# A hybrid decoder layer on one core: expert weights in a ring of ten 2 MB units, padding rows skipped, expert results scattered into the output by adding

## The chip, the cores and the metric

One core of one Trainium2 chip runs the whole layer in one launch. The metric is the device time in microseconds; three runs of the kernel before took 1293.37, 1296.27 and 1298.17 us, median 1296.27.

## The reference, cut to what matters

One layer over 512 prompt tokens and 8 sample tokens, model width 1024, all in float32. Projections, a pooling mixer, sparse attention and memory attention come first; the change touches what follows them:

```python
def finish(x, y_pool, o_nsa, o_mem, p):
    ...
    h = x + mixed @ p['w_out']
    hn = rmsnorm(h, p['g_ffn']).reshape(b * t, d)
    return h + hier_moe(hn, p).reshape(b, t, d)

def hier_moe(x, p):                      # top-1 of 4 groups, then top-2 of its 8 experts
    ...
    for gi in range(N_EXPERT_GROUPS):
        hg = jnp.einsum('nd,edf->nef', x, p['w_gate'][gi])
        hu = jnp.einsum('nd,edf->nef', x, p['w_up'][gi])
        h = jax.nn.silu(hg) * hu * combine[:, gi, :, None]
        y = y + jnp.einsum('nef,efd->nd', h, p['w_down'][gi])
    return y
```

Each of the 520 tokens goes to 2 of 32 experts, 1040 token-expert pairs in all, 32.5 an expert on average. An expert has three matrices, gate and up (1024 x 512) and down (512 x 1024), 2 MB each; the 32 experts have 201 MB.

## The kernel before

The kernel is a row of stages (`project`, `stream`, `attend`, `mix`, `experts`, `overflow`, `combine`), each a block in which every engine has its own program; the engines meet at a barrier at each stage's end (`close`). Within a stage the order on each engine is written out by hand and semaphores tie the engines.

`project` also clears the spare part of `ys_dram` with one 4 MB write of zeros from GpSimd's queue (L302). `mix` computes h and hn for five token tiles (four of 128, one of 8), stores them to `h_dram` and `hn_dram` (L1308, L1309), routes the tokens on VectorE, and makes `table` (slot by expert tile, the token in each slot; 64 slots a tile) by ten small matmuls (L1438) and one cast (L1660). Empty slots hold token 0. At its start SyncE loads the three matrices of expert 0 into `w_a` (L1297 to L1299), for the last token tile gate and up of expert 1 into `w_b` (L1306), and after the last logits its down matrix (L1317).

`experts` works on one expert n at a time with 64 rows:

- GpSimd gathers the 64 rows of hn into `xg` (L1726), one gather an expert, two buffers; gather n waits only for `x_turned` of n-2.
- TensorE runs, for each n: `gate_up(n)` (64 matmul passes, L1751), `turn_x(n+1)` (transposes of `xg`, L1739 and L1741), `down(n-1)` (16 passes, L1770), `turn_h(n)` (L1739, L1741).
- VectorE copies the transposes out (L1813, L1829) and computes the activation (L1819 to L1825), with ScalarE's exponential (L1856) between.
- ScalarE copies the result out of PSUM (L1862) and stores all 64 rows to `ys_dram` in two DMAs (L1865).
- SyncE loads gate and up of expert n+2 after the last up matmul of n, and down of n+2 after the last down matmul of n, into the half (`w_a` or `w_b`) that n leaves:

```python
sp.wait_ge(up_done, i * 4 + 2 * (slot - 1))
self.load_gate_up(sp, i * 2 + slot, slot, (wg[slot], wu[slot]))
sp.wait_ge(y_in_psum, i * 4 + 2 * (slot - 1))
self.load_down(sp, i * 2 + slot, slot, wd[slot])
```

`overflow` runs only if an expert has more than 64 rows, which these inputs don't have. `combine` gathers each token's two rows from `ys_dram` (ten gathers, L2020), multiplies each by its weight and adds it to h on VectorE (L2032, L2033), and stores the output (L2039).

Of the kernel before, what the change touches and what calls it, by code (L numbers as in the profile page):

```python
# [24 lines left out]
P = 128  # L25
# [3 lines left out]
NB = 8  # L29
# [34 lines left out]

C_ID = 0
# [16 lines left out]
CW = C_SEL + 16 * NB  # L82
# [7 lines left out]
def constants():  # L90
# [40 lines left out]
    c[:, C_TOK:C_TOK + 5] = i[:, None] + P * np.arange(5)[None, :]  # L131
    for u in range(2):
# [18 lines left out]
class Kernel:  # L151
# [35 lines left out]
    def project(self):  # L187
# [16 lines left out]
        xin2 = self.sb("xin", [P, 2, D], stack=st)  # L204
# [6 lines left out]
        blank = self.w1[0:CAP, :, :, :].rearrange("p a b c -> p (a b c)")[:, 0:D]  # L211
        blank_ready = self.sem("blank_ready", st)
# [33 lines left out]
        def _(sp):  # L246
# [21 lines left out]
            sp.wait_ge(self.blanked, 16)  # L268
# [28 lines left out]
        def _(pool):  # L297

            nc.gpsimd.memset(blank[:, :], 0.0).then_inc(blank_ready, 1)
            pool.wait_ge(blank_ready, 1)  # L300
            pool.wait_ge(win_in, 64)
            pool.dma_start(self.ys_dram[NEXP * CAP:, :].rearrange("(a p) d -> p a d", p=CAP), blank[:, :].unsqueeze(1).broadcast_to([CAP, NOVER, D])).then_inc(self.blanked, 16)  # L302
# [8 lines left out]
            pool.wait_ge(self.blanked, 16)  # L311
# [152 lines left out]
    def stream(self):  # L464
# [11 lines left out]
        XT = self.sb("XT", [P, 2, G, 512], stack=st)  # L476
# [55 lines left out]
        pTc = self.sb("pTc", [64, 64], stack=st)  # L532
# [427 lines left out]
    def attend(self):  # L960
# [15 lines left out]
        prob = self.sb("prob", [P, 2, 2, 512], stack=st)  # L976
# [275 lines left out]
    def mix(self):  # L1252
# [25 lines left out]
        place = self.sb("place", [P, 6, NT * 2], stack=st)  # L1278
        stored = [S(f"h_stored{j}") for j in range(2)]
        names = ("mix_dve", "cleared", "r_in_psum", "r_ready", "y_in_psum", "y_out", "ms_ready4", "root_ready", "mixed_ready",  # L1280
                 "mT_in_psum", "mT_ready", "h_in_psum", "hms", "hroot", "hn_ready", "hT_in_psum", "hT_ready", "l_in_psum",
                 "l_out", "lclear", "lexp", "pair_ready", "cnt_in_psum", "h_read", "h_copied", "hot_ready", "table_in_psum")
        (steps, cleared, r_in_psum, r_ready, y_in_psum, y_out, ms_ready, root_ready, mixed_ready,
         mT_in_psum, mT_ready, h_in_psum, hms, hroot, hn_ready, hT_in_psum, hT_ready, l_in_psum,
         l_out, lclear, lexp, pair_ready, cnt_in_psum, h_read, h_copied, hot_ready, table_in_psum) = (S(n) for n in names)
# [4 lines left out]
        tile_tok = mixed[:, 0, 0:2 * NT * NTILE].rearrange("p (n s) -> p n s", s=NTILE)  # L1290
# [4 lines left out]
        def _(sp):  # L1295

            wg, wu, wd = self.expert_slot(self.w_a)  # L1297
            self.load_gate_up(sp, 0, 0, (wg, wu))
            self.load_down(sp, 0, 0, wd)  # L1299
            for t in range(NT):  # L1300
                r = ROWS[t]
                if t == NT - 1:

                    wg, wu, wd = self.expert_slot(self.w_b)
# [12 lines left out]
            self.load_down(sp, 1, 1, wd)  # L1317

        @block.gpsimd
        def _(pool):  # L1320
            nc.gpsimd.memset(one[:, :, :, :], 0.0).then_inc(cleared, 1)
            nc.gpsimd.memset(cnt[:, :, :], 0.0).then_inc(cleared, 1)
            nc.gpsimd.memset(self.pair_w[:, :, :], 0.0).then_inc(cleared, 1)
            nc.gpsimd.memset(lg[:, :, :], 0.0).then_inc(cleared, 1)

        @block.tensor
        def _(pe):
# [3 lines left out]
            def windows(t):  # L1331
                r = ROWS[t]
                if t >= 1:
                    pe.wait_ge(r_ready, t)
                band = lambda w, j: bands[:, C_BAND + (3 * w + j) * P:C_BAND + (3 * w + j + 1) * P]
                for w in range(4):
                    u = z[0:r, t, U0 + 64 * w:U0 + 64 * w + 64]
# [343 lines left out]
    def experts(self):  # L1681
# [467 lines left out]
```

## Time and profile before

| what | us |
|---|---|
| median of three runs | 1296.27 (1293.37 to 1298.17) |
| span of the profiled execution, first to last instruction | 1288.5 |
| `experts` and later, from the first gather | 719.95 to 1288.5 |
| busy in the span: TensorE matmuls, VectorE, ScalarE, GpSimd | 1060.3, 458.5, 175.3, 71.2 |

The profiled execution has no time of its own beside its span; the median of the runs lies 7.8 us above the span, and that is taken as what lies around it. The weight loads run on queue q1 (SyncE's), ScalarE's stores on q10, GpSimd's gathers on q0; all three share the core's 16 DMA engines.

### The profile page before, as it was taken

Reading aid. Unit: us, or ns where it says so; the run is one execution under the profiler, and the core shown is the slowest. Engines: PE = TensorE matmul, PEld = TensorE weight load, DVE = VectorE, ACT = ScalarE, POOL = GpSimd, SP = SyncE. Lnnn points to the kernel's source line nnn. Section 1 sums busy time; section 2 is a strip of 40 time slices with the busy share of each in tenths; the row PEclk is TensorE's granted clock in tenths of the full one; section 3 lists DMA queues with packets and bytes.
Section 4 is the critical chain, followed back from the end, with each engine's and each line's share of the span. In section 5 each row is a group of like instructions: output and inputs, shape, how many; then the busy total and the mean of one; then the engine's idle time right before and its main releaser. Section 6 shows DMA issues by size and latency. Waiting matters only on the chain. (4 is left out here: it accounts for less than half of the span.)

```text
span 1288.5 us, 16001 instructions
## 1 busy us (share of the span) xinstructions
PE 1060.3 (82%) x6275; PEld 694.2 (54%) x6275; DVE 458.5 (36%) x950; ACT 175.3 (14%) x415; POOL 71.2 (6%) x104
## 2 busy tenths in 40 slices
PE   5899979999996899988996498788887788877880
PEld 2455657777784677776455354444444444444440
DVE  3233313422424678653434322222222222222223
ACT  1021211111100344330001000000000000000000
POOL 0000030100100000000000100000000000000003
PEclk9999889999976799686996698999999999999995
DMA  9970083553100600004115279999999999999995
GB/s 396 266 231 25 13 199 99 154 141 98 50 1 2 253 1 1 1 1 196 69 63 231 81 284 401 403 400 408 409 404 407 405 407 410 406 413 415 407 382 207
DMA packets 58438, 294.33 MB, mean 228 GB/s; under 512 B 6992, under 2 KB 23183, under 8 KB 40783
## 3 DMA queue, kind: packets, MB, share of 16 engines
q1 hardware_dynamic: 35191, 255.76, 51.8%
q0 software_dynamic: 5280, 21.15, 5.2%
q10 hardware_dynamic: 17920, 16.78, 4.2%
q8 instruction: 31, 0.51, 0.2%
q14 instruction: 16, 0.13, 0.0%
HBM read 272.55 MB, written 25.42 MB: 231 GB/s over the span
## 5 line engine op out<-in xcount | busy, mean ns | idle before, releaser
L1751 PE MATMUL ps<-w_b,xTe 128*64 128x256 f32 x1024 | 132.0, 416 | 37.8 <-DMA w_b<-in_w_up 34.1
L1751 PE MATMUL ps<-w_a,xTe 128*64 128x256 f32 x1024 | 123.2, 397 | 27.0 <-DMA w_a<-in_w_up 24.9
L1813 DVE COPY xTe<-ps 128x512 f32<-128x512 f32 x32 | 22.1, 692 | 345.9 <-PE ps L1741 345.9
L829 PE MATMUL ps<-XT,w_a 128*128 128x126 f32 (+1 forms) x576 | 132.9, 409 | 5.7 <-DVE ht L564 5.7
L829 PEld LDWEIGHTS ps<-XT,w_a 128*128 128x128 f32 x576 | 120.4, 227 | 15.4 <-issue 6.3
L1751 PEld LDWEIGHTS ps<-w_b,xTe 128*64 128x64 f32 x1024 | 81.4, 150 | 83.9 <-DMA w_b<-in_w_up 40.9
L1751 PEld LDWEIGHTS ps<-w_a,xTe 128*64 128x64 f32 x1024 | 74.3, 142 | 71.3 <-DMA w_a<-in_w_up 30.8
L430 PE MATMUL ps<-w_b,xT 128*128 128x454 f32 (+1 forms) x240 | 81.1, 549 | 0.7 <-ACT z L402 0.7
L1856 ACT ACTIVATE gc<-gc 128x256 f32<-128x256 f32 x32 | 13.3, 416 | 450.2 <-DVE gc L1819 450.2
L1726 POOL DMA_INDIRECT xg<-hn_dram,table x32 | 28.8, 899 | 592.6 <-PE ps L1741 453.9
L1378 PE MATMUL ps<-w_b,mT 128*128 128x512 f32 x128 | 58.1, 614 | 1.9 <-ACT mT L1446 1.3
L430 PEld LDWEIGHTS ps<-w_b,xT 128*128 128x128 f32 (+1 forms) x240 | 38.0, 172 | 39.7 <-issue 39.7
L1770 PE MATMUL ps<-w_b,hTe 128*64 128x512 f32 x256 | 58.5, 599 | 0.5 <-DVE hTe L1829 0.5
L1770 PE MATMUL ps<-w_a,hTe 128*64 128x512 f32 x256 | 58.4, 598 | 0.0
L1822 DVE RECIPROCAL gc<-gc 128x256 f32<-128x256 f32 x32 | 56.1, 1753 | 1.1
L1098 PEld LDWEIGHTS ps<-z,pT 128*128 128x128 f32 x320 | 40.9, 207 | 15.9 <-ACT pT L1238 10.2
L1098 PE MATMUL ps<-z,pT 128*128 128x64 f32 x320 | 43.7, 293 | 3.3 <-DVE pT L1204 3.1
L1739 PE MATMUL ps<-consts,hh 128*128 128x128 f32 x64 | 16.4, 338 | 34.8 <-DVE hh L1825 34.8
L1739 PEld LDWEIGHTS ps<-consts,hh 128*128 128x128 f32 x64 | 10.2, 199 | 62.2 <-DVE hh L1825 61.3
L1378 PEld LDWEIGHTS ps<-w_b,mT 128*128 128x128 f32 x128 | 24.8, 197 | 32.6 <-issue 30.9
L550 DVE COPY KsT<-ps 128x512 f32<-128x512 f32 x8 | 5.5, 692 | 101.6 <-PE ps L806 101.6
L1227 ACT ACTIVATE prob<-ps,stt 128x256 f32<-128x256 f32 (+3 forms) x80 | 40.4, 522 | 2.7 <-DVE stt L1159 2.6
(362 smaller groups left out, 1308.5 us busy)
## 6 DMA issues: line engine op xcount, KB each, us to landing
w_a<-in_w_gate SPq DMA_DIRECT2D x16, 2048.0 KB, 17.2
w_a<-in_w_up SPq DMA_DIRECT2D x16, 2048.0 KB, 23.3
w_a<-in_w_down SPq DMA_DIRECT2D x16, 2048.0 KB, 12.5
w_b<-in_w_gate SPq DMA_DIRECT2D x16, 2048.0 KB, 16.6
w_b<-in_w_up SPq DMA_DIRECT2D x16, 2048.0 KB, 22.4
w_b<-in_w_down SPq DMA_DIRECT2D x16, 2048.0 KB, 13.2
w_a<-in_cache_kv SPq DMA_DIRECT2D x64, 256.0 KB, 5.1
ys_dram<-yb ACTq DMA_DIRECT2D x64, 128.0 KB, 7.8
```

Source lines behind the costliest of these rows:

```text
L430: ins = nc.tensor.matmul(in_psum(t, a), xT[:, t % 2, k, 0:r], rhs, start=(k == 0), stop=(k == KD - 1))
L829: ins = nc.tensor.matmul(hidv[:, 2 * q:2 * q + 2, 0:n], w1[:, q, l, :], XT[:, q, :, l:l + 8 * (n - 1) + 1:8], start=(l == 0), stop=(l == 15))
L1098: ins = nc.tensor.matmul(ps[:, 6, 64 * c:64 * c + 64], pT[:, j, at:at + 128], z[:, k, v:v + 64], **add)
L1227: ins = nc.scalar.activation(pr[:, i // n, i % n, :], sc[:, i // n, i % n, :], ACT.Exp, bias=stt[:, u % 2, 1, i:i + 1], scale=SCALE, accum ...
L1378: ins = nc.tensor.matmul(ps[0:r, 4 + a, :], mT[:, k, 0:r], w_out[:, k, 512 * a:512 * a + 512], start=(k == 0), stop=(k == KD - 1))
L1726: pool.indirect_dma_start(out=xg[:, n % 2, :], out_offset=None, in_=self.hn_dram, in_offset=bass.IndirectOffsetOnAxis(ap=self.table[:, n:n ...
L1739: ins = nc.tensor.matmul(dst, src, ident, start=True, stop=True)
L1751: ins = nc.tensor.matmul(ps[h * CAP:h * CAP + CAP, bank, 0:FH], xT[:, slot, k, :], w[slot][:, k, h * FH:h * FH + FH], start=(k == 0), stop ...
L1770: ins = nc.tensor.matmul(ps[a * CAP:a * CAP + CAP, 6 + slot, :], hT[:, j, h * CAP:h * CAP + CAP], wd[slot][:, h, j, 512 * a:512 * a + 512] ...
L1813: nc.vector.tensor_copy(xT[:, slot, :, :].rearrange("p k s -> p (k s)"), ps[:, 4, 0:KD * CAP]).then_inc(xT_ready, 1)
L1822: link(nc.vector.reciprocal(gc[:, slot, :], gc[:, slot, :]), n * 3 + 2)
L1856: nc.scalar.activation(gc[:, slot, :], gc[:, slot, :], ACT.Exp, scale=-1.0).then_inc(ge_ready, 1)
```

## The change

Five things are changed together.

1. **Ring of units.** `w_a`, `w_b`, the former `z` and 4 MB more make ten units of 2 MB; unit u = 3n + m holds matrix m (gate, up, down) of expert n and lies in place u mod 10. Each unit is loaded as soon as the unit ten before it has been read. `mix` loads units 0, 1, 2, 6, 7 at its start (6 and 7 lie where z was, so GpSimd first copies 256 columns of z to `zu`, and TensorE's first matmuls and these loads wait for it), 3 and 4 at the last token tile, 5 after the last logits; `experts` loads 8 and 9 at once.
2. **Padding.** Empty slots of the table hold 2048, beyond the bound that the gather is given, so their rows aren't fetched. Slot 0 of a tile always has a row.
3. **Scatter.** ScalarE multiplies the result by the slot's weight as it copies it out of PSUM (the weights come out of the same, now doubled, table matmuls). GpSimd adds it into the output by one indirect DMA an expert, 128 half rows of 2 KB with a bound that leaves the empty slots out. `mix` stores h straight to the output.
4. **Order on GpSimd.** For each n: wait for `x_turned` of n, gather n+2, wait for `y_copied` of n and for scatter n-1 to have landed, scatter n. The first two gathers stand in `mix`.
5. **Gone**: `combine`, `ys_dram` and its clearing in `project`, the stores on ScalarE's queue, `h_dram`. `overflow` is folded into `experts`.

```diff
@@ project @@
-            pool.dma_start(self.ys_dram[NEXP * CAP:, :].rearrange("(a p) d -> p a d", p=CAP), blank[:, :].unsqueeze(1).broadcast_to([CAP, NOVER, D])).then_inc(self.blanked, 16)
@@ mix @@
-            self.load_gate_up(sp, 0, 0, (wg, wu))
-            self.load_down(sp, 0, 0, wd)
+            for u in range(3):
+                self.load_unit(sp, u)
+            sp.wait_ge(u_kept, 2)
+            for u in range(6, 8):
+                self.load_unit(sp, u)
...
-                    self.load_gate_up(sp, 1, 1, (wg, wu))
+                    for u in range(3, 5):
+                        self.load_unit(sp, u)
...
-                sp.dma_start(self.h_dram[t * P:t * P + r, :], h[0:r, t % 2, :]).then_inc(stored[t % 2], 16)
+                sp.dma_start(O["y"][t * P:t * P + r, :], h[0:r, t % 2, :]).then_inc(stored[t % 2], 16)
...
-            self.load_down(sp, 1, 1, wd)
+            self.load_unit(sp, 5)
...
+            nc.gpsimd.tensor_copy(zu[:, 0:TILES, :], z[:, 0:TILES, U0:U0 + 256]).then_inc(u_kept, 1)
+            nc.gpsimd.tensor_copy(zu[0:NB, TILES, :], z[0:NB, TILES, U0:U0 + 256]).then_inc(u_kept, 1)
...
+            pool.wait_ge(table_ready, 1)
...
+            for n in range(2):
+                self.gather(pool, n)
...
-                    ins = nc.tensor.matmul(ps[0:CAP, 0, 0:NTILE], slot_hot[0:r, n, :], tile_tok[0:r, n, :], start=(n == 0), stop=(n == 2 * NT - 1))
+                    for a in range(2):
+                        ins = nc.tensor.matmul(ps[CAP * a:CAP * a + CAP, 0, 0:2 * NTILE], slot_hot[0:r, n, :], tile_hot[0:r, n, :, :].rearrange("p m s -> p (m s)"),
+                                               start=(n == 0), stop=(n == 2 * NT - 1))
...
+            ch.then(nc.vector.tensor_tensor(weighted, hot, pw[:, :, :].rearrange("p t k -> p (t k)").unsqueeze(2).broadcast_to([P, 2 * NT, NTILE]), ALU.mult))
+            nc.vector.scalar_tensor_tensor(hot, tok[:, :].unsqueeze(2).broadcast_to([P, 2 * NT, NTILE]), -float(FAR), hot, ALU.add, ALU.mult).then_inc(hot_ready, 1)
...
+            ch.then(nc.vector.tensor_scalar(row, ps[:, 0, 0:NTILE], float(FAR), self.c(C_LAST, 1), ALU.add, ALU.min))
+            nc.vector.tensor_copy(self.table[:, :], row[0:CAP, :]).then_inc(table_ready, 1)
+            nc.vector.tensor_scalar(self.halves[:, :], row, 2.0, self.c(C_HALF, 1), ALU.mult, ALU.add)
+            nc.vector.tensor_copy(self.slot_w[:, :], ps[:, 0, NTILE:2 * NTILE])
@@ experts @@
+    def gather(self, pool, n):
+
+        pool.indirect_dma_start(out=self.xg[0:CAP, n % 2, :], out_offset=None, in_=self.hn_dram,
+                                in_offset=bass.IndirectOffsetOnAxis(ap=self.table[:, n:n + 1].bitcast(U32), axis=0),
+                                bounds_check=NTOK - 1, oob_is_err=False).then_inc(self.xg_in[n % 2], 16)
...
+        def scatter(pool, n, slot, sem):
+
+            pool.indirect_dma_start(out=rows, out_offset=bass.IndirectOffsetOnAxis(ap=self.halves[:, n:n + 1].bitcast(U32), axis=0),
+                                    in_=yb[:, slot, :], in_offset=None, bounds_check=2 * NTOK - 1, oob_is_err=False,
+                                    compute_op=ALU.add).then_inc(sem, 16)
...
+            for u in range(8, NU):
+                if u >= RING:
+                    n, m = (u - RING) // 3, (u - RING) % 3
+                    if m == 0:
+                        sp.wait_ge(gate_done, 2 * n + 2)
+                    elif m == 1:
+                        sp.wait_ge(up_done, 2 * n + 2)
+                    else:
+                        sp.wait_ge(y_in_psum, 2 * n + 2)
+                self.load_unit(sp, u)
...
             for n in range(NEXP):
-                if n >= 2:
-                    pool.wait_ge(x_turned, n - 1)
-                pool.indirect_dma_start(out=xg[:, n % 2, :], out_offset=None, in_=self.hn_dram,
-                                        in_offset=bass.IndirectOffsetOnAxis(ap=self.table[:, n:n + 1].bitcast(U32), axis=0)).then_inc(xg_in[n % 2], 16)
+                if n + 2 < NEXP:
+                    pool.wait_ge(x_turned, n + 1)
+                    self.gather(pool, n + 2)
+                pool.wait_ge(y_copied, n + 1)
+                if n >= 1:
+                    pool.wait_ge(y_out, 16 * n)
+                scatter(pool, n, n % 2, y_out)
...
+                nc.scalar.activation(yb[:, n % 2, :], ps[0:2 * CAP, 6 + n % 2, :], ACT.Copy, scale=self.slot_w[:, n:n + 1]).then_inc(y_copied, 1)
```

TensorE's order in `experts` stays, `down(n)` now waits for `y_copied` of n-2 only, and the loops are unrolled.

## Rows read from the trace of the kernel before

**Rows 1.** Windows: length, busy us of each engine, TensorE clock, DMA share, GB/s.
```profile
40.00:60.00 20.00, 20.00 (x54) 10.53 (x53) 3.78 (x8) 1.38 (x3) 0.00 (x0) 0.92 1.00 237
...
719.00:757.00 38.00, 26.78 (x175) 16.21 (x175) 8.94 (x14) 1.42 (x3) 4.59 (x5) 0.78 0.42 146
757.49:1225.57 468.08, 377.90 (x2578) 213.73 (x2577) 121.43 (x196) 28.03 (x56) 24.18 (x27) 0.96 1.01 406
1264.00:1288.50 24.50, 0.00 (x0) 0.00 (x0) 12.73 (x10) 0.00 (x0) 10.27 (x10) 0.50 0.73 261
```

**Rows 2.** Waits from 760 to 1240 us: waiter, releaser, total us, times, longest.
```profile
POOL xg L1726 <- PE ps L1741: 425.3, 27, 18.9
...
PE ps L1751 <- DMA w_b<-in_w_up: 32.8, 14, 3.1
...
PE ps L1751 <- DMA w_a<-in_w_up: 24.9, 13, 2.9
```

**Rows 3.** DMA queues from 760 to 1240 us: packets, MB, share of 16 engines.
```profile
q1 hardware_dynamic: 16068, 180.76, 92.7%
q0 software_dynamic: 2160, 7.08, 4.3%
q10 hardware_dynamic: 4640, 7.61, 4.2%
```

**Rows 4.** Timeline, TensorE and ScalarE passes of `experts`: start us, us, instruction.
```profile
752.28 3.65 PE L1770 MATMUL ps<-w_a,hTe 128*64 128x512 f32 x16
...
1225.57 7.13 PE L1751 MATMUL ps<-w_a,xTe 128*64 128x256 f32 x64
...
1232.62 0.69 PE L1739 MATMUL ps<-consts,xg 64*128 64x64 f32 x2
...
1234.00 3.65 PE L1770 MATMUL ps<-w_b,hTe 128*64 128x512 f32 x16
...
1237.72 0.58 ACT L1862 COPY yb<-ps 128x512 f32<-128x512 f32 x1 [2.15 <-PE ps L1770]
...
1238.66 0.50 PE L1739 MATMUL ps<-consts,hh 128*128 128x128 f32 x2 [1.00 <-DVE hh L1825]
...
1253.11 3.65 PE L1770 MATMUL ps<-w_b,hTe 128*64 128x512 f32 x16 [0.52 <-DVE hTe L1829]
```

**Rows 5.** Line 707, GpSimd copies of 128x512 elements: ns min/median/max.
```profile
L707 POOL COPY kvc<-w_a x34: 599/613/801, 166.6 to 349.7; 128x512 f32<-128x512 f32 x34
```

**Rows 6.** Timeline, end of `mix`: the table and the first gather.
```profile
715.52 2.53 PE L1438 MATMUL ps<-mixed 128*64 128x48 f32 x20 [9.31 <-DVE mixed L1647]
...
718.16 0.20 DVE L1660 CAST table<-ps 64x48 int32<-64x48 f32 x1 [0.86 <-PE ps L1438]
719.95 0.99 POOL L1726 DMA_INDIRECT xg<-hn_dram,table  x1 [138.39 <-POOLq L171]
```

**Rows 7.** Tile xg, 719 to 730 us: landing of three gathers without weight loads.
```profile
DMA to landing us min/median/max: 3.7/3.8/3.8
```

**Rows 8.** Timeline of SyncE's queue, end of `mix` and start of `experts`.
```profile
694.33 0.40 SPq L1678 DMA_DIRECT2D w_b<-in_w_down  x1
734.96 0.38 SPq L1674 DMA_DIRECT2D w_a<-in_w_gate  x1
...
756.01 0.38 SPq L1678 DMA_DIRECT2D w_a<-in_w_down  x1
```

**Rows 9.** Tile xg, 760 to 1240 us: its gathers and their landing (ns; us).
```profile
L1726 POOL DMA_INDIRECT xg<-hn_dram,table x27: 895/895/898, 766.3 to 1202.1; - x27
...
DMA to landing us min/median/max: 8.7/8.9/9.6
```

**Rows 10.** DMA queues from 1006.5 to 1008.5 us, amid one gather.
```profile
q1 hardware_dynamic: 32, 0.52, 81.6%
q0 software_dynamic: 32, 0.13, 19.2%
```

**Rows 11.** Tile rows: landing of `combine`'s ten gathers, no weight loads beside them.
```profile
DMA to landing us min/median/max: 4.6/6.1/7.7
```

More of the change, by code:

```diff
@@ L62 @@
 QMAX = (NTOK - 1) // CAP
+UNIT = KD * FF
+RING = 10
 C_ID = 0
@@ L131, in constants @@
     c[:, C_TOK:C_TOK + 5] = i[:, None] + P * np.arange(5)[None, :]
+    c[:, C_HALF] = i >= CAP
+    c[:, C_LAST] = np.where(i % CAP == 0, NTOK - 1, FAR)
     for u in range(2):
@@ L1585, in _ @@
             nc.vector.tensor_tensor(both[:, :, :], one[:, :, 0, :], one[:, :, 1, :], ALU.add).then_inc(pair_ready, 1)
-            pw = self.pair_w
+            for k in range(2):
+                nc.vector.tensor_copy(tok[:, k:2 * NT:2], self.c(C_TOK, NT))
             dve.wait_ge(lexp, 1)
@@ L1690, in experts @@
         FH = FF // 2
-        wg, wu, wd = zip(self.expert_slot(self.w_a), self.expert_slot(self.w_b))
-        xg = self.sb("xg", [CAP, 2, D], stack=st)
+        more = self.sb("more", [P, RING - 8, UNIT], stack=st)
+        self.units += [more[:, j, :] for j in range(RING - 8)]
         xT = self.sb("xTe", [P, 2, KD, CAP], stack=st)
-        gc = self.sb("gc", [2 * CAP, 2, FF // 2], stack=st)
-        hh = self.sb("hh", [2 * CAP, 2, FF // 2], stack=st)
+        gc = self.sb("gc", [2 * CAP, 2, FH], stack=st)
@@ L1754, in gate_up, with turn_x, down @@
                                 ins.then_inc(done, 1)
-            def turn_x(n, slot, half, first=False):
-                pe.wait_ge(xg_in[slot], half * 16)
-                if not first:
+            def turn_x(n):
+                pe.wait_ge(xg_in[n % 2], 16 * (n // 2 + 1))
+                if n >= 1:
                     pe.wait_ge(xT_ready, n)
-                turn(4, xg[:, slot, :], KD).then_inc(x_turned, 1)
-            def down(n, slot, half, first=False):
+                turn(4, xg[0:CAP, n % 2, :], KD).then_inc(x_turned, 1)
+            def down(n):
                 pe.wait_ge(hT_ready, n + 1)
-                pe.wait_ge(d_in[slot], half * 16)
-                if not first:
-                    pe.wait_ge(y_copied, n)
+                arrived(3 * n + 2)
+                wd = self.down_half(3 * n + 2)
+                if n >= 2:
+                    pe.wait_ge(y_copied, n - 1)
                 for k in range(KF):
@@ L1773, in down, with turn_h @@
                             ins.then_inc(y_in_psum, 1)
-            def turn_h(n, slot):
+            def turn_h(n):
                 pe.wait_ge(hh_ready, n + 1)
-                turn(5, hh[:, slot, :], KF // 2).then_inc(h_turned, 1)
-            turn_x(0, 0, 1, first=True)
-            gate_up(0, 0, 1)
-            turn_x(1, 1, 1)
-            turn_h(0, 0)
-            gate_up(1, 1, 1)
-            turn_x(2, 0, 2)
-            down(0, 0, 1, first=True)
-            turn_h(1, 1)
-            with pe.Fori(1, NEXP // 2 - 1) as i:
-                for slot in range(2):
-                    n = i * 2 + slot
-                    gate_up(n, slot, i + 1)
-                    turn_x(n + 1, 1 - slot, i + 1 + slot)
-                    down(n + (-1), 1 - slot, i + slot)
-                    turn_h(n, slot)
@@ L1794, in _ @@
-            n, half = NEXP - 2, NEXP // 2
-            gate_up(n, 0, half)
-            turn_x(n + 1, 1, half)
-            down(n - 1, 1, half - 1)
-            turn_h(n, 0)
-            gate_up(n + 1, 1, half)
-            down(n, 0, half)
-            turn_h(n + 1, 1)
-            down(n + 1, 1, half)
+                turn(5, hh[:, n % 2, :], KF // 2).then_inc(h_turned, 1)
+            turn_x(0)
+            for n in range(NEXP):
+                gate_up(n)
+                if n + 1 < NEXP:
+                    turn_x(n + 1)
+                if n >= 1:
+                    down(n - 1)
+                turn_h(n)
```

433 lines of the change are left out of this document (168 added, 265 removed).

## The prediction

> **What bounds the kernel now.** I read the windows first, by stage. From 757.49 to 1225.57 us, 28 experts, the 16 DMA engines are busy all the time (share 1.01, 406 GB/s), while TensorE is busy 377.9 of 468.1 us [rows 1]: 16.72 us an expert, and the DMA sets it. The waits agree: TensorE's idle time in this stretch is mostly the wait for the up matrix, 57.7 us over 27 times, and GpSimd waits 425 us in all, so its gathers come with time to spare [rows 2]. The queues say what fills the DMA: over 480 us (28.7 experts) q1, the weights, takes 92.7%, which is 15.5 us an expert; q0, the gathers, 4.3% or 0.72 us; q10, the stores, 4.2% or 0.70 us [rows 3]. Two stretches beside it are not full: from 719 to 757 the DMA share is 0.42, and after the last down matmuls (1256.76 by [rows 4]) 31.7 us go by until 1288.5 with almost nothing but `combine` [rows 1].
>
> TensorE's own pace is the second thing to read [rows 4]. With the weights there, 64 gate and up passes take 7.1 us; turn_x takes 1.37 us until down starts (1232.62 to 1234.00); down 3.65; then about 1.0 us of waiting for hh and 0.9 us of turn_h until the next expert. That sums to about 14.7 us with the gaps between.
>
> **The change, part by part.** I build the end as: end of the first down pass, plus 29 times the period T of the experts, plus what follows.
>
> *The start.* GpSimd's copy of z (1024 columns; copies of 512 columns take 0.61 us [rows 5], so 1.2, and the small one with its semaphore) delays the first matmuls of `mix` by 1.7 us. The added VectorE step on 480 columns costs about 0.7 us, an estimate from ScalarE's 0.58 for 512 columns [rows 4]. The table's matmuls double, 2.53 us for 20 [rows 6], so +2.5; one more short step before the table's cast +0.25. Against that the first gather no longer waits for the barrier: 718.36 to 719.95, -1.6 [rows 6]. Sum +3.6; down(0), which ended at 755.93 [rows 4], ends at 759.6. Doubled work on the table's other outputs lies beside the gather's landing (3.8 us [rows 7]). The clearing of `ys_dram` I cost at nothing: it lay at about 40 to 60 us, where TensorE was busy without a break (20.0 of 20 us [rows 1]), and SyncE's next loads were not waited for.
>
> *The weights' head start.* Before, only six units were in by 719; units 6 and 7 were issued at 734.96, the next at 756.01 [rows 8]. Now twelve are in by then: units 6 and 7 come in `mix`, 8 and 9 at 720, 10 and 11 behind the first gate and up. From 761 on, 84 units remain.
>
> *Bytes.* An expert's gather falls to half, 0.36 us on average; if the valid rows, which lie in the first slots, all go to the same half of the engines, those keep 0.72. The scatter moves 65 half rows instead of 128. Before shows no adding DMA. Below, it costs as plain stores, 0.36 us; above, it also reads its destination, as gathers read, another 0.36. So 16.2 to 16.9, and by the share of 1.01, 16.0 to 16.7 us an expert; I take 16.35, as a read cannot come free, 5.45 a unit. If the DMA alone decided, the last up matrix would be in at 761 + 83 x 5.45 = 1213, down(31) done 12 us later (up 3.6, down(30) 3.65, turn_h and its copy 1.3, down 3.65 [rows 4]) at 1225.
>
> *The new chain on GpSimd.* Gather n+3 now stands behind scatter n, and scatter n waits for the copy of down n. TensorE wants gather n+3 for turn_x(n+3), which stands ahead of down(n+1). So there is a loop from down(n) to down(n+1):
> - end of down to end of the copy, 0.65 us (1237.65 to 1238.30 [rows 4]), and 0.3 until GpSimd issues, as for other issues
> - L, from the scatter's issue to the landing of the gather behind it
> - 0.1 wake, turn_x 1.37, down 3.65.
>
> T = 6.07 + L. Before, gathers were issued a whole pass ahead and their landing didn't matter; it took 8.9 us beside the weights [rows 9] and 3.8 without them [rows 7]. The difference is read from 1006.5 to 1008.5: in 2 us, 32 packets of q1 and 32 of q0 [rows 10]. That is one each per engine and microsecond: every 4 KB row waits for one 16 KB weight packet, 1.0 us a turn, and a gather of 64 rows has four turns. The rest of its landing is 8.9 - 4.0 = 4.9 us beside the weights, and 3.0 without (3.8 less four bare rows of 0.19: q0's 4.3% of 480 us on 16 engines, over its 27 x 64 rows).
>
> Now scatter and gather share q0, one behind the other. L is: the fixed part, 3.0 to 4.9, I take 4.0, as the weights pause near the end of down when T is over 16.35; the scatter's 65 half rows, 4 an engine, and its closing packet, 5 turns of 0.7 (short packet) to 1.0, I take 0.95, since it reads memory too; the gather's rows, 2 turns if spread over 16 engines, 4 if the first slots are on eight, I take 3 of 1.0. L = 4.0 + 4.75 + 3 = 11.75, T = 17.8. Lowest: 3.0 + 3.5 + 2 = 8.5, T = 14.6. Highest: 4.9, nine turns of 1.0 (an engine may hold 8 slots of a full expert), 4: 17.9, T = 24. GpSimd's second issue (0.9 us [rows 9] and 0.3) hides behind the scatter's turns, and scatter n-1 has landed long before. The stall of TensorE that follows keeps the DMA from being full: what was a wait for the up matrix becomes a wait for xg, and the head start lies unused in the ring.
>
> *The end.* After down(29) come turn_h, gate_up(31), down(30), turn_h, down(31): 1.8 + 7.3 + 3.7 + 0.8 + 5.0 = 18.6 us. Then copy 0.95 with the wake, a scatter of 128 slots, as a gather of that size lands in 4.6 at best [rows 11], and 0.3 to finish: 5.8. Before this tail took 31.7, so 26 us are saved whatever T is.
>
> Sum: 759.6 + 29 x 17.8 + 18.6 + 5.8 = 784 + 516.2 = 1300.2 us span, 11.7 more than 1288.5. With the 7.8 us around it (median less span) that is **1308 us**, slower by 0.9%. The break-even is T = 17.4; each 0.1 us of T is worth 2.9 us.
>
> *A rule on the queues.* The turns above come from [rows 10]. The Trainium skill, page "DMA: Bandwidth & Descriptors", section "Queues, rings and completion order", says that an engine goes round the queues a packet at a time and empties a packet of some 9 to 17 descriptors before it switches. By it a scatter's four rows an engine would go in one turn, as would the gather's. The trace disagrees for the gathers of 4 KB rows, with one row to each weight packet; for 2 KB half rows on q0 no row here shows it.
>
> **The rivals.**
>
> *A, faster: the loop is short enough.* It decides from T = 15.4 down, where 784 + 29T meets the end by the DMA, 1225 + 5.8 = 1231. For it: the lowest bounds above give 14.6. Against: all three would have to hold at once. Time 1231 + 7.8 = 1239, 4.4% faster. Chance 16%.
>
> *B, faster: one turn for each DMA.* If all of an engine's rows of one DMA go in one turn, a turn is one weight packet, 0.82 (81.6% of 2 us on 16 engines over 32 packets), and four rows of 0.19: 1.6 us. L = 4.0 + 3.2 = 7.2, T = 13.3, and the DMA decides again: 1239 too. Against it stand [rows 10]. This is the packet rule of the skill's page cited above. Chance 4%.
>
> *C, faster by less: T from 15.4 to 17.2*, with two gather turns, or a fixed part near 3.0. At 16.3: 784 + 472.7 + 7.8 = 1264, 2.4% faster. Chance 22%.
>
> *D, much slower: T above 20.* The empty slots still take turns in the queue (8 + 1 for the scatter, 4 for the gather: L = 4.0 + 8.6 + 4 = 16.6, T = 22.7), so the padding isn't really gone, or an adding packet takes far more than a store. At 22.7: 784 + 658 + 8 = 1450. Nothing in the trace speaks for or against. Chance 14%.
>
> **How the numbers follow.** My forecast, T from 17.2 to 20, has 44%: 1291 to 1372. A measurement of this kernel can tell about 0.5% (6.5 us) from no change; that is T from 17.2 to 17.6, 8% of these 44, the rest slower. So faster 16 + 4 + 22 = 42%, same 8%, slower 36 + 14 = 50%. The range takes in A (the low edge 1236) and reaches to T = 20, 784 + 580 + 8 = 1372; outside are D and a little below A. The forecast's own range is 1291 to 1372.
>
> **What would show it.** In the profile after: GpSimd's indirect DMAs in pairs, scatter then gather, some 1.2 us apart, right behind each copy of yb; TensorE's turn_x waiting for the DMA of xg, 2 to 5 us an expert, and no wait for the up matrix; DMA share near 0.93 in the expert stretch; landing of xg over 8 us from its own issue; packets of q0 one to one with weight packets; no `combine`, a tail near 6 us; down(0) ending near 760. The forecast fails if xg lands less than 9 us after down ends (then A or B: waits for weights stay, and the DMA is full), or if q0 shows as many packets as before (D).

## The result, and the profile after

The kernel after takes 1455.79 us (median of 4 runs, 1447.87 to 1456.26) against 1297.22 us (median of 4, 1293.37 to 1299.05): ratio 1.119 [1.1135, 1.125], slower by 12%. The forecast was 1308 us, range 1236 to 1372. The course that came is the one called D, and its own working gave 1450.

Executions of one kernel differ by up to 2%, and a profile shows one of them: of e1 and e5 below it is the shortest (1252.39 and 1247.57 us), of e6 the longest (1283.39 us).

The windows of the kernel after, over 400 us of experts, show neither TensorE nor the DMA full. Columns as in [rows 1], where the DMA share was 1.01 at 406 GB/s:

```profile
800.00:1200.00 400.00, 253.95 (x1579) 134.16 (x1581) 75.56 (x123) 19.17 (x35) 43.08 (x34) 0.79 0.76 288
```

The waits from 780 to 1430 us say who is late, beside [rows 2]:

```profile
POOL out_y L1741 <- ACT yb L1950: 573.7, 29, 21.3
...
PE ps L1810 <- DMA xg<-hn_dram,table: 230.7, 28, 9.2
```

No wait for a weight matrix is left. TensorE stands before turn_x for 8.2 us an expert (230.7 / 28), where it stood 57.7 us in all for the up matrices before. The timeline of one expert (start us, us, instruction, idle before and releaser) shows the loop, from the end of one down to the end of the next:

```profile
1010.51 5.77 PE L1847 MATMUL ps<-w_b,hTe 128*64 128x512 f32 x16
...
1016.35 0.33 SPq L1698 DMA_DIRECT2D w_b<-in_w_gate  x1
1016.35 0.69 ACT L1950 ACTIVATE yb<-ps,slot_w 128x512 f32<-128x512 f32 x1 [4.26 <-PE ps L1847]
...
1016.72 0.43 SPq L1698 DMA_DIRECT2D z<-in_w_up  x1
...
1017.19 0.43 SPq L1701 DMA_DIRECT2D z<-in_w_down  x1
1017.86 1.55 POOL L1741 DMA_INDIRECT out_y<-yb,halves  x1 [20.39 <-ACT yb L1950]
1019.72 0.98 POOL L1705 DMA_INDIRECT xg<-hn_dram,table  x1 [0.30 <-issue]
...
1032.45 0.74 PE L1810 MATMUL ps<-consts,xg 64*128 64x64 f32 x2 [8.57 <-DMA xg<-hn_dram,table]
...
1033.88 6.03 PE L1847 MATMUL ps<-more,hTe 128*64 128x512 f32 x16
```

Down ends at 1016.28, the copy at 1017.04, the scatter is issued at 1017.86, the gather at 1019.72; turn_x starts at 1032.45, down ends at 1039.91: 23.63 us. The mean of the 29 periods is 22.63. The landing of both DMAs from their own issue (us), for yb and then for xg:

```profile
DMA to landing us min/median/max: 4.0/11.7/13.4
...
DMA to landing us min/median/max: 3.4/12.3/13.4
```

Before, the median for xg was 8.9, in [rows 9]. The chain that ended last says the same of the whole span: 24% of it is the gather's way into `xg`, 11% is down.

```profile
DMA xg<-hn_dram,table 24%; PE ps L1847 11%; POOL out_y L1741 3%; PE ps L1827 2%; PE ps L1810 2%; PE ps L1812 2%; ACT yb L1950 1%; DMA out_y<-yb,halves 0%; DVE gc L1905 0%; DVE xTe L1895 0%; POOLq L1741 0%; DVE hh L1908 0%; DVE gc L1906 0%; ACT gc L1944 0%; POOLq L1705 0%
```

Three more things are in these rows that the forecast did not have. Down takes 5.8 to 6.0 us, not the 3.65 of [rows 4]. SyncE issues three units in one burst right behind down. And between, the DMA runs empty. The windows around those lines show the clock and the DMA share (last three columns: granted clock, share, GB/s):

```profile
1010.51:1014.50 3.99, 3.99 (x11) 1.24 (x12) 3.33 (x5) 0.42 (x1) 0.00 (x0) 0.50 0.21 86
1014.50:1016.28 1.78, 1.78 (x9) 0.36 (x5) 0.58 (x2) 0.00 (x0) 0.00 (x0) 0.92 0.00 0
1017.00:1023.80 6.80, 6.80 (x64) 4.31 (x60) 0.28 (x1) 0.04 (x1) 2.54 (x2) 1.00 0.96 343
1024.00:1032.40 8.40, 0.00 (x0) 0.00 (x0) 0.00 (x0) 0.00 (x0) 0.00 (x0) 0.77 1.00 382
```

The last line is the wait for the next expert's rows, 8.4 us in which TensorE does nothing. Behind such a wait and the short turn_x, down runs at 0.50 of the clock, that is 1.2 GHz, for its first 4 us, and only its last part gets 2.4 GHz back (0.92 is the mean of that window).

The queues, from 780 to 1430 us (packets, MB, share of 16 engines), against [rows 3]:

```profile
DMA packets 21950, 180.47 MB, mean 278 GB/s; under 512 B 4951, under 2 KB 4951, under 8 KB 7831
...
q1 hardware_dynamic: 15420, 172.18, 68.2%
q0 software_dynamic: 6504, 7.90, 5.6%
```

The 6504 packets of q0 belong to 29 scatters and 28 gathers (and a piece of one more of each). With every slot as a packet and a closing packet on each engine, a scatter has 128 + 16 and a gather 64 + 16: 224 a pair, 6504 / 224 = 29.0 pairs. With the empty slots gone it would be 65 + 16 and 32.5 + 16, or 29.0 x 129.5 = 3756. The bytes are those of the real rows alone: 29 x 65 x 2 KB + 28 x 32.5 x 4 KB = 7.6 MB. So an empty slot moves nothing, and is still a packet. One gather's time, 1019 to 1031 us, shows the two queues side by side:

```profile
q1 hardware_dynamic: 337, 4.41, 90.0%
q0 software_dynamic: 220, 0.25, 9.9%
```

Per engine that is 13.8 packets of q0 and 21 of q1. Course D had 9 + 4 packets in this place; it left out the one that closes the gather.

### The profile page after: what moved, and what is told of

Read it like the earlier page. It is cut to its first block and busy times, and to the rows that moved or that the text cites. A ratio compares the mean times of both kernels' runs of the same rounds, so it can differ in the third digit from the quotient of the medians.

```text
span 1454.1 us, 15378 instructions
## 1 busy us (share of the span) xinstructions
PE 1100.9 (76%) x6295; PEld 700.5 (48%) x6295; DVE 446.8 (31%) x944; ACT 178.8 (12%) x415; POOL 112.9 (8%) x125
## 5 line engine op out<-in xcount | busy, mean ns | idle before, releaser
L1810 PE MATMUL ps<-consts,xg 64*128 64x64 f32 x64 | 23.4, 464 | 237.4 <-DMA xg<-hn_dram,table 230.7
L831 PE MATMUL ps<-xg,w_a 128*128 128x126 f32 (+1 forms) x576 | 131.9, 407 | 5.9 <-DVE ht L566 5.9
L831 PEld LDWEIGHTS ps<-xg,w_a 128*128 128x128 f32 x576 | 118.7, 222 | 16.2 <-issue 6.4
L1741 POOL DMA_INDIRECT out_y<-yb,halves x32 | 49.7, 1554 | 618.9 <-ACT yb L1950 615.6
L1827 PE MATMUL ps<-w_a,xTe 128*64 128x256 f32 x640 | 73.8, 388 | 0.8 <-DVE xTe L1895 0.8
L1827 PE MATMUL ps<-w_b,xTe 128*64 128x256 f32 x640 | 74.3, 390 | 0.0
L1394 PE MATMUL ps<-w_b,xg 128*128 128x512 f32 x128 | 58.2, 614 | 1.9 <-ACT xg L1464 1.3
L1827 PEld LDWEIGHTS ps<-w_b,xTe 128*64 128x64 f32 x640 | 46.1, 141 | 24.5 <-issue 2.6
L1827 PEld LDWEIGHTS ps<-w_a,xTe 128*64 128x64 f32 x640 | 45.9, 140 | 24.9 <-issue 1.7
L1827 PE MATMUL ps<-z,xTe 128*64 128x256 f32 x384 | 43.3, 381 | 0.0
L1827 PE MATMUL ps<-more,xTe 128*64 128x256 f32 x384 | 43.3, 381 | 0.0
## 6 DMA issues: line engine op xcount, KB each, us to landing
w_b<-in_w_up SPq DMA_DIRECT2D x10, 2048.0 KB, 14.7
```

The source lines that it names most:

```text
L831: ins = nc.tensor.matmul(hidv[:, 2 * q:2 * q + 2, 0:n], w1[:, q, l, :], XT[:, q, :, l:l + 8 * (n - 1) + 1:8], start=(l == 0), stop=(l == 15))
L1394: ins = nc.tensor.matmul(ps[0:r, 4 + a, :], mT[:, k, 0:r], w_out[:, k, 512 * a:512 * a + 512], start=(k == 0), stop=(k == KD - 1))
L1741: pool.indirect_dma_start(out=rows, out_offset=bass.IndirectOffsetOnAxis(ap=self.halves[:, n:n + 1].bitcast(U32), axis=0), in_=yb[:, slot, ...
L1810: ins = nc.tensor.matmul(dst, src, ident, start=True, stop=True)
L1827: ins = nc.tensor.matmul(ps[h * CAP:h * CAP + CAP, bank, 0:FH], xT[:, slot, k, :], w[:, k, h * FH:h * FH + FH], start=(k == 0), stop=(k == ...
```

## The experiments

All are compared with the kernel before, run beside them on the same chips (medians 1294.35, 1298.95 and 1294.92 us for e1 to e4, e5 to e8, e9 to e11). The stages ahead of the experts vary from one profile to the next with code that is the same: `mix` began at 580.8 us in the profile before, at 587.9 in the one after and at 575.8 in that of e1. So small differences are read in the *stretch*, from the first gather's issue to the end of the span: 568.5 us before, 724.0 after. The stretch is that of the profiled execution alone, so among e1, e5, e6 and e11, which lie close together, the medians are read beside it. The *period* is the mean distance of the scatters from that of expert 5 to that of expert 25: 16.72 before (28 experts of [rows 1]), 23.04 after.

| run | median us | ratio [95%] | stretch | period |
|---|---|---|---|---|
| before | 1297.22 | 1 | 568.5 | 16.72 |
| after | 1455.79 | 1.119 [1.1135, 1.125] | 724.0 | 23.04 |
| e1 gather ahead of the scatter | 1264.52 | 0.980 [0.974, 0.986] | 532.0 | 16.37 |
| e2 all 64 rows gathered | 1483.02 | 1.149 [1.142, 1.156] | 751.8 | 23.90 |
| e3 plain write | 1394.04 | 1.079 [1.072, 1.085] | 662.2 | 20.83 |
| e4 loads in the order of release | 1428.68 | 1.105 [1.098, 1.112] | 700.3 | 22.36 |
| e5 e1 and e4 | 1261.92 | 0.971 [0.967, 0.975] | 531.7 | 16.40 |
| e6 e1 with a ring of six | 1272.79 | 0.977 [0.972, 0.982] | 550.0 | 16.73 |
| e7 TensorE busy in the wait, 28 passes | 1547.86 | 1.191 [1.186, 1.197] | 818.9 | 25.92 |
| e8 gather of 32 slots | 1432.48 | 1.100 [1.093, 1.107] | 704.6 | 22.25 |
| e9 as e7, 16 passes | 1418.77 | 1.096 [1.086, 1.106] | 695.6 | 21.45 |
| e10 no scatter | 1276.64 | 0.988 [0.982, 0.995] | 546.2 | 16.74 (gathers) |
| e11 e1 and e2 | 1280.76 | 0.992 [0.988, 0.997] | 557.8 | 17.51 |

**e1: the gather goes ahead of the scatter.** On GpSimd, in iteration n, and with n = 0 fetching expert 2 as well:

```diff
-                if n + 2 < NEXP:
-                    pool.wait_ge(x_turned, n + 1)
-                    self.gather(pool, n + 2)
+                if n + 3 < NEXP:
+                    pool.wait_ge(x_turned, n + 2)
+                    self.gather(pool, n + 3)
```

> Only GpSimd's order changes: gather n+3 is issued when turn_x(n+2) is done, ahead of scatter n, instead of behind it. Loop theory (the period of 22.6 us is copy, scatter, gather behind it, turn_x, down): the gather has a whole pass of slack again, the waits for xg vanish, down takes 3.65 us again instead of 5.8, and the DMA sets the period at 16.6 to 17.2 us; time 1255 to 1275 us. Rival (the adding scatter and its packets slow the DMA itself, whatever the order): the period stays above 20 us, time above 1380.

Measured 1264.52 us, 2.0% faster than before and 13% faster than after, from moving one instruction past one wait. (The code lets gather n+3 go when turn_x(n+1) is done, not turn_x(n+2) as the expectation says.) On the queue a gather still stands right behind a scatter:

```profile
1015.13 1.55 POOL L1741 DMA_INDIRECT out_y<-yb,halves  x1 [11.86 <-ACT yb L1953]
1016.98 0.98 POOL L1705 DMA_INDIRECT xg<-hn_dram,table  x1 [0.30 <-issue]
```

But it is now the gather that TensorE needs one expert later, so the same chain of copy, scatter, gather, turn_x and down spans two experts instead of one. Down takes 3.65 us again (109.5 us for 480 passes from 780 to 1400 us). The window and the queues of e1 (800 to 1200, 780 to 1200 us):

```profile
800.00:1200.00 400.00, 336.79 (x2283) 199.09 (x2281) 105.23 (x171) 26.89 (x49) 62.44 (x50) 0.94 1.02 398
```

```profile
q1 hardware_dynamic: 14173, 159.27, 93.7%
q0 software_dynamic: 5941, 7.32, 7.5%
```

The DMA is full again. The 16.37 us are a mean of two paces, though. The first eight scatters after expert 0's follow each other at 13.6 us, the pace of TensorE with its weights at hand, while the ring's head start is used up; from expert 9 to 29 the mean is 17.02 us, with TensorE waiting for gate and up matrices. Scatters of e1 at either pace:

```profile
812.78 1.55 POOL L1741 DMA_INDIRECT out_y<-yb,halves  x1 [10.80 <-ACT yb L1953]
826.42 1.55 POOL L1741 DMA_INDIRECT out_y<-yb,halves  x1 [10.80 <-ACT yb L1953]
...
1033.03 1.55 POOL L1741 DMA_INDIRECT out_y<-yb,halves  x1 [15.07 <-ACT yb L1953]
1051.65 1.55 POOL L1741 DMA_INDIRECT out_y<-yb,halves  x1 [15.79 <-ACT yb L1953]
```

A gather still takes 12.9 us to land (median), but it has a whole expert's time more for it: the order, not the landing, is what costs. The packets of q0 are about as many an expert as in the kernel after.

**e2: all slots fetch a row.** Empty slots of the table get token 519 instead of none.

```diff
-            nc.vector.tensor_copy(self.table[:, :], row[0:CAP, :]).then_inc(table_ready, 1)
+            nc.vector.tensor_scalar(self.table[:, :], row[0:CAP, :], float(NTOK - 1), None, ALU.min).then_inc(table_ready, 1)
```

> Empty slots gather row 519 instead of being out of bounds, so that each gather moves 64 real rows; the scatter is left as it is. If an out-of-bounds slot still puts a packet into the queue and takes a turn (padding theory), nothing is saved by skipping it: 1456 us, up to 15 more for the rows' own 0.19 us. If skipped slots take no turn, a gather now has two turns an engine more, of 0.8 to 1.0 us each in the loop: 1500 to 1515 us.

27.8 us in the stretch, 0.9 us a period; the landing went from 12.3 to 13.2 us. That lies between the two expectations (up to 15 us, or 44 and more), but the packets decide: q0 has 3871 of them in 420 us, 220 a period of 23.90, as many as with the rows skipped. The empty slots of the gather save their bytes and not their packets. What the bytes cost was put too low: 0.9 us for two rows more on each engine, 0.45 us a row, not 0.19.

**e3: a plain write in the scatter.** The output then has neither h nor any but one of each token's shares.

```diff
-                                    in_=yb[:, slot, :], in_offset=None, bounds_check=2 * NTOK - 1, oob_is_err=False,
-                                    compute_op=ALU.add).then_inc(sem, 16)
+                                    in_=yb[:, slot, :], in_offset=None, bounds_check=2 * NTOK - 1, oob_is_err=False).then_inc(sem, 16)
```

> The scatter writes instead of adding, so the output lacks h and all but one expert's share of a row; the packets' number and order stay. Loop theory by turns: a half row's own time falls from 0.18 to about 0.09 us, at most 8 turns, 0.4 to 0.8 us of the period: 1432 to 1445 us. Rival (the adding itself is what is slow): below 1380 us.

61.8 us less in the stretch, and 1394.04 us, outside both expectations: too much for a change of the rows' own time, too little for the rival. The scatters of e3 on GpSimd (ns min/median/max), their landing, and q0 from 780 to 1200 us:

```profile
L1741 POOL DMA_INDIRECT out_y<-yb,halves x31: 994/1015/1021, 794.0 to 1384.5; - x31
...
DMA to landing us min/median/max: 2.4/7.9/10.2
```

```profile
q0 software_dynamic: 3258, 5.35, 3.7%
```

3258 packets in 420 / 20.83 = 20.2 periods are 161 a pair, where adding had 224: the 128 half rows of a plain write go two to a packet (64 + 16 + 64 + 16 = 160). GpSimd spends 1.02 us on the issue instead of 1.55, the write lands 3.8 us sooner, and the gather behind it 1.3 us sooner (11.0). So the adding form, with its packet for each slot and its longer issue, costs 2.2 us of the loop. That the number of packets would stay, as expected, was wrong; how much is the adding itself and how much the packets, e3 can't tell. The write's own empty slots are still packets.

**e4: the loads in the order in which their places come free.** In the kernel after SyncE takes the units in the order of their numbers, so a wait for a down matrix's place holds back the gate and up behind it.

```diff
-            for u in range(8, NU):
+            freed = lambda u: ((u - RING) // 3 + ((u - RING) % 3 == 2), (u - RING) % 3)
+            for u in list(range(8, RING)) + sorted(range(RING, NU), key=freed):
```

> Only SyncE's order changes: the loads are issued in the order in which their places come free (gate, up of n+1 before down of n), instead of three in a burst right after down(n), where scatter and gather are issued too. Loop theory: the same number of turns, each still behind a weight packet for most of the time, but less of a queue ahead of the first packet and a DMA that isn't idle before: period 0 to 2 us shorter, 1400 to 1456 us. Rival (the burst is the cause): period below 19 us, under 1350.

23.7 us less in the stretch. The timeline of e4 shows the burst gone:

```profile
1015.85 0.33 SPq L1698 DMA_DIRECT2D w_b<-in_w_gate  x1
1017.37 1.55 POOL L1741 DMA_INDIRECT out_y<-yb,halves  x1 [19.18 <-ACT yb L1951]
1019.22 0.98 POOL L1705 DMA_INDIRECT xg<-hn_dram,table  x1 [0.30 <-issue]
1020.00 0.33 SPq L1698 DMA_DIRECT2D more<-in_w_up  x1
1023.45 0.38 SPq L1701 DMA_DIRECT2D w_a<-in_w_down  x1
```

The time is in the expected range, and the rival (under 1350) is out. The gather's median landing falls from 12.3 to 12.0 us and the scatter's from 11.7 to 11.1. The period falls by 0.7 us: in the timelines turn_x starts 0.5 us sooner after the gather's issue, on average, and the time from there to the end of down is 0.2 us shorter. Over 20 periods that is 13.6 us, and 7.1 more lie in one period near the end (16.1 us instead of 23.2). It is a cost that no term of the prediction had; that it acts through three units standing in the queue at once is the likely reading and not shown by itself.

**e5: e1 and e4 together.** 

> Gather ahead of the scatter, as in e1, and the loads in the order in which places come free, as in e4. With the DMA full the order of the loads can only fill the gap near the start (746 to 768 us in the profile after): 4 to 10 us below e1, 1255 to 1261 us. If the burst still matters when the gather has slack: below 1245 us.

Its stretch is 531.7 us against e1's 532.0, its median 2.6 us lower, less than the 4 to 10 expected. With the DMA full, the order of the loads is worth nothing that these runs show clearly.

**e6: e1 with six places instead of ten.** `RING = 6`, units 6 to 9 are not loaded ahead, and z and the 4 MB more are not used.

> e1 with a ring of six units instead of ten: no units 6 to 9 ahead, loads as early as a place among six allows. If the head start of four units is what the ring is worth, the same period and 4 x 5.5 = 22 us more than e1: about 1286 us. If a deeper ring also smooths waits within a period: above 1300 us. If the ring is worth nothing: 1265 us.

Its median is 8.3 us above e1's, but the kernel before was 4.6 us slower beside it too, and the ratios, 0.977 and 0.980, overlap. So in whole runs the six places cost nothing that is clear of noise. The stretches, 18 us apart, are of executions of 1283.39 and 1252.39 us and can't settle it. Within the traces the head start can be seen: e6 has two short periods, of 14.0 and 14.6 us, where e1 has eight of 13.6, and from the first scatter to that of expert 9 it needs 20.4 us more, near the 22 expected. From expert 9 to 29 it is a little quicker, 16.82 us a period against 17.02. In the kernel after the ring is worth nothing, as it never waits for a weight.

**e7 and e9: the clock.** In the wait for xg, TensorE does passes on constants into a PSUM part that nothing reads, 28 of them an expert in e7 and 16 in e9:

```diff
-                pe.wait_ge(xg_in[n % 2], 16 * (n // 2 + 1))
...
+                if n >= 3:
+                    for k in range(28):
+                        nc.tensor.matmul(ps[:, 4, 0:256], self.consts[:, C_ID:C_ID + P], self.consts[:, 0:256], start=True, stop=True)
+                pe.wait_ge(xg_in[n % 2], 16 * (n // 2 + 1))
```

> The kernel after the change, and 28 matmuls without use (128x256, about 6.2 us) in each wait for xg, so that TensorE isn't idle before turn_x and down. If the fall of the granted clock in that wait costs part of the loop (down 5.8 us instead of 3.65, turn_x a little), the period falls by 2.2 to 2.5 us: 1385 to 1400 us. If down is long for another reason, or isn't in the loop: 1456 us or more.

e7 missed its aim. The timeline and the window of e7:

```profile
1000.61 12.35 PE L1837 MATMUL ps<-consts 128*128 128x256 f32 x56
...
1014.27 3.65 PE L1850 MATMUL ps<-w_a,hTe 128*64 128x512 f32 x16
```

```profile
800.00:1200.00 400.00, 384.27 (x2272) 274.77 (x2270) 68.69 (x111) 17.55 (x32) 37.98 (x30) 1.00 0.66 249
```

One matmul of 128 rows shows as two passes in the profile (x56 for 28) and takes 0.44 us, twice what the 64-wide ones suggested, so 28 took 12.35 us and overran a wait of 8.4. The time, 1547.86 us, thus says nothing on either expectation. It still shows what it was made for: the granted clock is 1.00, and down takes 3.65 us again. e9 repeats it at the right length.

> As e7, with 16 matmuls without use instead of 28: in e7 they took 12.35 us and overran the wait for xg of 8.4 us; 16 take 7.1 us and end before the rows land. If the fallen clock costs 2.2 to 2.5 us of the loop: from the first gather to the end 724 - 29 x 2.3 = 657 us, time 1380 to 1400 us. If the clock is not part of the loop: 724 us, 1456.

```profile
1016.50 0.69 PE L1810 MATMUL ps<-consts,xg 64*128 64x64 f32 x2 [1.75 <-DMA xg<-hn_dram,table]
...
1017.87 3.65 PE L1850 MATMUL ps<-more,hTe 128*64 128x512 f32 x16
```

The stretch falls by 28.4 us, less than half of the 67 expected, the period by 1.6 (2.3 expected). Over 780 to 1400 us down takes 4.0 us on average (117.5 us for 470 passes, in the lines by form) where the kernel after has 5.67 (153.1 us for 432): 1.7 us, not 2.2. The gather's landing rose from 12.3 to 12.6 us. In some experts the passes reach to the end of the wait and just delay turn_x, and before the last turn_x, where the kernel after doesn't wait, they cost 8 us of the stretch (a period of 20.7 instead of 12.6). So the clock's fall is a consequence of the wait that adds 1.0 to 1.6 us to the period; it does not make the loop.

**e8: a gather of 32 slots.** The rows in slots 32 to 63 stay as they were in `xg`; 14 of the 32 experts have some.

```diff
-        pool.indirect_dma_start(out=self.xg[0:CAP, n % 2, :], out_offset=None, in_=self.hn_dram,
-                                in_offset=bass.IndirectOffsetOnAxis(ap=self.table[:, n:n + 1].bitcast(U32), axis=0),
+        m = CAP // 2
+        pool.indirect_dma_start(out=self.xg[0:m, n % 2, :], out_offset=None, in_=self.hn_dram,
+                                in_offset=bass.IndirectOffsetOnAxis(ap=self.table[0:m, n:n + 1].bitcast(U32), axis=0),
```

> The kernel after the change with gathers of 32 slots instead of 64; rows of experts in slots 32 to 63 are left out (14 of the 32 experts have some). If each slot, empty or not, is a packet that waits its turn, an engine has two packets fewer, 1.0 to 1.6 us of the loop, and a few real rows less: 1405 to 1428 us. If empty slots cost nothing, only the full experts gain: 1445 us or more.

Two packets fewer on each engine gave 19.4 us of the stretch and 23.3 of the median, 0.7 to 0.8 us a period where 1.0 to 1.6 were expected; the time, 1432.48 us, is 4 us above the range. That is 0.33 to 0.40 us a packet (19.4 or 23.3 / 29 / 2), with some real rows left out too. A turn in the gather's part of the loop is much cheaper than the 1.0 us of [rows 10].

**e10: the scatter left out.** GpSimd waits as before for the copy, then only raises the semaphore; the output is h alone.

```diff
-                scatter(pool, n, n % 2, y_out)
+                pool.sem_inc(y_out, 16)
```

> The kernel after the change without the scatter; GpSimd still waits for each copy of yb before the next gather, so the output is h alone. Loop theory: the gather no longer stands behind nine turns of the scatter, it lands some 9 us after the copy, and the loop is 0.8 + 0.8 + 9 + 1.5 + 3.7 = 15.8, up to 17.6 us with a fallen clock: from the first gather to the end 520 to 570 us, time 1250 to 1300 us. Rival (waiting for the copy before the gather is by itself what costs, with or without the scatter): period above 19 us, time above 1340 us.

The stretch falls by 178 us, to 546.2. The gather lands in 8.6 us (median), near the 8.9 of [rows 9]. One period of e10 in the timeline:

```profile
1010.21 0.69 PE L1810 MATMUL ps<-consts,xg 64*128 64x64 f32 x2 [2.79 <-DMA xg<-hn_dram,table]
...
1011.63 5.21 PE L1847 MATMUL ps<-z,hTe 128*64 128x512 f32 x16
```

The wait for the copy alone keeps a stall of 2.8 us and the slow clock in down (0.50 from 1011.63 to 1014.00 us), yet the DMA is nearly full (q1 94.5%). The rest of the loss, from 546 to 724 us, comes with the scatter between the copy and the gather: its issue (1.86 us), its packets ahead of the gather's, and the longer waits of TensorE that follow.

**e11: e1 with e2's edit.** 

> e1 (gather ahead of the scatter) with gathers of 64 real rows, as e2. Here the DMA sets the period, so what counts is busy time: 31.5 rows of 0.19 us on 16 engines, 0.37 us an expert: 9 to 12 us from the first gather to the end, against 27 us in e2, where the same rows stood in the loop. Time 1270 to 1278 us. If skipping is worth nothing when the order is right: 1264 us.

Measured 1280.76 us, above the range: 16.2 us more than e1 by the medians, 25.8 in the stretch. So in a full DMA 31.5 more rows an expert cost 0.5 to 0.8 us, or (16 x 0.5 or 0.8 / 31.5) 0.26 to 0.41 us a row on its engine, more than the 0.19 that the share of q0 in [rows 3] gives. The queues from 780 to 1200 us, beside those of e1 above:

```profile
q1 hardware_dynamic: 13334, 150.28, 91.8%
q0 software_dynamic: 5600, 9.87, 9.5%
```

At the weights' pace (6.29 MB an expert) that is 17.58 us an expert instead of 16.59. q0's own busy time rises by 0.43 us, from 7.5% of 16.59 to 9.5% of 17.58, which is 0.22 us a row; the weights' rises too, by 0.6, for the same bytes. That the gather leaves out its padding is thus worth 0.5 to 0.8 us an expert with the loop gone, and 0.9 within it (e2).

## Why the prediction was wrong, point by point

The mechanism was right: the loop from down to down through GpSimd's order, the wait for xg in place of the wait for up, the unused head start in the ring, the slower side. **The step that failed is the size of L**, "the scatter's 65 half rows, 4 an engine, and its closing packet, 5 turns [...]; the gather's rows, 2 turns if spread over 16 engines [...], I take 3", which counted the empty slots as taking no turn. L was put at 11.75 us and measured 14.2 (1.86 to the gather's issue, 12.3 to its landing). The packets of q0 and e2 show the empty slots as packets; e10 shows that the gather lands 3.7 us sooner with no scatter ahead of it, e3 1.3 sooner with fewer packets ahead. The price of an empty slot was measured on the gather alone (e8); no run leaves out only the scatter's. By e8's 0.33 to 0.40 us for each of the six empty slots an engine has (four of the scatter, two of the gather) they would be worth 2.0 to 2.4 us, an estimate, against the 2.45 by which L was short.

**A second step failed beside it: down at 3.65 us in the loop**, which measured 5.67, as the wait itself brought the clock down. With L alone put right the forecast would be 784 + 29 x 20.25 + 7.8 = 1379 us, with down alone 1367; only both together come near the result.

| term of the sum | forecast | measured |
|---|---|---|
| down(0) ends | 759.6 | 768.3 |
| L | 11.75 | 14.2 |
| end of down to the scatter's issue | 0.95 | 1.58 |
| wake and turn_x | 1.47 | 1.5 |
| down in the loop | 3.65 | 5.67 |
| T | 17.8 | 22.63 |
| 29 T | 516.2 | 656.1 |
| down(29) to down(31) | 18.6 | 16.8 |
| tail after the last down | 5.8 | 12.9 |
| span | 1300.2 | 1454.1 |

- *L.* Of the 4.8 us by which T was short, 2.4 are L, 2.0 down, the rest the copy and the wake. The bounds given for L, 8.5 to 17.9, held it. The trace has 13.8 packets of q0 an engine, 9 + 5, at (14.2 - 4.0) / 14 = 0.73 us a turn, an estimate, if the fixed part is the 4.0 taken. D's own count was 9 + 4, but it put L at 16.6, and the unforeseen 2 us in down filled the gap. So D's 1450 us is nearer than its working deserves, by luck. That q0's packets would be "one to one with weight packets" did not hold either: 220 to 337.
- *Down at 3.65 us.* Taken from rows in which TensorE hardly waited. With a wait of 8 us an expert the granted clock was down at the start of each down, 2.0 us; e7 and e1 show it return, and e9 prices it net at 1.0 to 1.6.
- *GpSimd's wake* was 0.82 us after the copy, not 0.3: +0.5.
- *The order of SyncE's loads* was not thought of: the loads of gate and up stand in unit order behind the wait for down's place. By e4 it costs 23.7 us of the stretch, 0.7 us a period, most of it in the gather's landing.
- *The start.* Between the start of `mix` and the first gather 142.3 us went by, 139.2 before: +3.1, forecast +3.6. Down(0) ends 12.3 us later than in [rows 4]: 7.1 of it lie ahead of `mix` (587.9 against 580.8), in code that the change hardly touches (e1, with that same code, is at 575.8, so this is how executions differ), and 2.1 between the first gather and down(0).
- *The bytes.* 16.35 us an expert was forecast for a DMA that decides, of 16.0 to 16.7. That the period of e1 is 16.37 is luck, as it is the mean of 13.6 and 17.0. By the bytes of its q1, 159.27 MB in 420 us, the DMA needed 16.6 us an expert, within the range and at its upper end. q0's share says why: the gather costs 0.45 us (2.7% of 16.74 in e10), 0.36 was put, and the scatter 0.8 (7.5% of 16.59 in e1, less the gather), 0.36 to 0.72 was put. TensorE's own pace, added up to 14.7 from [rows 4], is 13.6.
- *The tail.* Saved were 19 us, not 26. The last down ends at 1441.24, the last scatter is issued at 1442.92 (it waits for the one before to land, 0.7 us more than forecast) and lands in 3.7 us, where 4.6 was forecast. Then 7.4 us go by in which the windows show no engine busy and next to no transfer; the forecast had 0.3 for it:

```profile
1447.00:1454.10 7.10, 0.00 (x0) 0.00 (x0) 0.00 (x0) 0.00 (x0) 0.00 (x0) 0.50 0.00 1
```

  e1 ends with the same 7 us. What still stands there in the code is the engines' test whether `overflow` has to run, now part of `experts`; no run leaves it out, so the cause stays open.
- *Around the span* lie 1.9 us (1456.0 for the execution of 1454.1), not 7.8, and 1.8 for the kernel before in its later runs; the rest is how the profiled execution before lay in its runs.
- *The packet rule* of the Trainium skill ("DMA: Bandwidth & Descriptors", "Queues, rings and completion order"), rival B, would have made the whole scatter one turn and the time 1239. The trace of the kernel after does not agree: it counts 144 packets for a scatter, 9 on each engine, the scatter lands in 11.7 us, and taking two packets off each engine in e8 shortened the loop.
- *The chance.* D had 14%, for "nothing in the trace speaks for or against". One number did: [rows 3] has 2160 packets for 27 gathers, 80 each, one to each slot and 16 to close, so a slot was known to be a packet. The open question was only whether a bound takes the packet away, and that deserved an even chance. The prediction's own sign for D, as many packets on q0 as before, was the right one to watch.

What stays open: how the clock's 2.0 us in down and the 1.0 to 1.6 of e9 go together in full, and how a packet's price in L divides between real, empty and closing ones (e8 gives 0.33 to 0.40 us for two of the last slots, the mean is 0.73).

## What to carry to other kernels

When a new step is put on an engine's queue, write down what already stood there and what it now waits for: here a gather that nobody waited for came to stand behind a wait for the previous expert's result and behind that expert's scatter, which closed a loop through the latency of two DMAs, and moving it one place forward turned 12% slower into 2.0% faster. The latency of a DMA under load, not its bytes, is the price of a link in such a loop. Count its packets by slot, ask what clock an engine will have behind the wait that a loop gives it, and try the order in which loads are issued only where the DMA is not full.

## What the runs showed of the hardware

- An indirect DMA with a bound makes a packet for each slot, in or out of the bound (224 a scatter and gather in the kernel after, 220 with all rows fetched in e2); one out of it carries next to nothing but takes its turn (e8: 0.33 to 0.40 us of the loop for each, with some real rows among them).
- An adding scatter of 2 KB rows has a packet for each slot and 1.55 us of GpSimd; a plain one puts two in a packet and takes 1.02. Under load they land in 11.7 and 7.9 us.
- A gathered 4 KB row costs 0.26 to 0.41 us of an engine when the DMA is full (e11 against e1), more than the 0.19 to 0.22 of its share of busy time.
- After 8.4 us without work and a turn_x of 1.4 us, TensorE runs down at 0.50 of its clock (1.2 GHz) for 4 us: 16 passes of 512 columns take 5.8 to 6.1 us instead of 3.65. In e10 a wait of 2.8 us stood before one that took 5.21.
